# A two-block transformer kernel: modulation sums in column groups, and the pooling bias in one pass

## The reference, cut to what matters

```python
sc = jax.nn.silu(c)                                   # 1024 numbers
for i in range(DEPTH):                                # 2 layers
    mod = (sc @ ada_w[i] + ada_b[i]).reshape(B, N_MOD, D_MODEL)   # 9 x 1024
    x = modulated_sublayer(x, mod[:, 0:3], ..., swiglu ...)
    x = modulated_sublayer(x, mod[:, 3:6], ..., pool_mixer or mla_mixer ...)
    x = modulated_sublayer(x, mod[:, 6:9], ..., swiglu ...)

def modulated_sublayer(x, mod, g_pre, g_post, fn, weight):
    shift, scale, gate = mod[:, 0], mod[:, 1], mod[:, 2]
    h = rmsnorm(x, g_pre) * (1.0 + scale) + shift
    y = rmsnorm(fn(h), g_post)
    return x + weight * (1.0 + gate) * y
```

```python
y = jnp.einsum('bsgc,gcd->bsgd', pooled - hg, w) + b      # w (4,256,256), b (4,256)
return y.reshape(B, S, D_MODEL) * scale
```

## Time and profile before

| | |
|---|---|
| median of 3 runs | 1593.99 us (1592.29 to 1594.13) |
| the profiled execution, whole | 1589.41 us |
| its span, first to last instruction | 1587.6 us |
| busy in the span | PE 97%, DVE 78%, ACT 54%, POOL 5% |
| mean granted TensorE clock | 0.995 of full |
| chain that ended last | PE 88%, DVE 5%, ACT 4%, DMA 1%, issue 1% |

### The profile page before, as it was taken

One profiled execution on the slowest core, in us unless ns is written; L12 is line 12 of the kernel. 1 busy time (PEld: TensorE's weight loads), 2 busy tenths in 40 slices (PEclk: granted clock), 3 DMA queues, 4 the chain that ended last, 5 costly groups with the idle time before them and its releaser, 6 DMA issues.

```text
span 1587.6 us, 19436 instructions
## 1 busy us (share of the span) xinstructions
PE 1544.1 (97%) x7573; PEld 1255.5 (79%) x7573; DVE 1230.4 (78%) x1800; ACT 854.9 (54%) x1245; POOL 79.5 (5%) x135
## 2 busy tenths in 40 slices
PE   7999999999999999999999999899999999999998
PEld 3888886888888888877888888777788888787876
DVE  2898877988868888664486654759888799989896
ACT  3544445544445344456454543555567567777774
POOL 1110100000001000000011000000001000000000
PEclk9999999999999999999999999899999999999999
DMA  9999856988857988323267554345323569989893
GB/s 346 375 379 350 287 191 206 334 300 305 299 174 256 323 285 309 129 89 107 86 236 219 175 179 163 108 133 186 132 106 103 186 213 352 348 312 350 317 341 126
DMA packets 196338, 373.76 MB, mean 235 GB/s; under 512 B 8986, under 2 KB 102608, under 8 KB 196240
## 3 DMA queue, kind: packets, MB, share of 16 engines
q1 hardware_dynamic: 176688, 301.08, 55.0%
q0 software_dynamic: 18864, 69.76, 12.6%
q10 hardware_dynamic: 688, 1.62, 0.3%
HBM read 371.38 MB, written 1.05 MB: 235 GB/s over the span
## 4 chain that ended last, share of the span: by engine, by line
PE 88%; DVE 5%; ACT 4%; DMA 1%; issue 1%; SPq 0%; POOL 0%; DVEq 0%; ACTq 0%
PE banks L524 25%; PE banks L526 24%; PE banks L525 24%; DVE ul L460 1%; PE banks L1586 1%; PE banks L1067 1%; PE banks L635 1%; PE banks L1559 1%; ACT uh L449 1%; PE banks L2116 1%; DMA raw<-in_ffn_w_in 1%; PE banks L1573 1%; PE banks L2718 1%; ACT arena L762 1%; DVE full L1005 1%; PE banks L936 1%
## 5 line engine op out<-in xcount | busy, mean ns | idle before, releaser
L449 ACT ACTIVATE uh<-raw 128x1024 fp32r<-128x1024 f32 (+2 forms) x548 | 569.0, 1049 | 408.1 <-PE banks L526 403.3
L460 DVE TENSOR_TENSOR ul<-raw,uh 128x1024 fp32r<-128x1024 f32 (+2 forms) x548 | 656.8, 1209 | 163.3 <-ACT uh L449 155.3
L524 PE MATMUL banks<-uh,hh 128*128 128x512 f32 (+2 forms) x1296 | 514.7, 397 | 12.9 <-DVE hl L1011 8.1
L526 PE MATMUL banks<-uh,hl 128*128 128x512 f32 (+2 forms) x1296 | 502.9, 388 | 0.0
L525 PE MATMUL banks<-ul,hh 128*128 128x512 f32 (+2 forms) x1296 | 501.8, 387 | 0.0
L524 PEld LDWEIGHTS banks<-uh,hh 128*128 128x128 f32 x1296 | 244.3, 189 | 68.3 <-DVE hl L1011 11.5
L526 PEld LDWEIGHTS banks<-uh,hl 128*128 128x128 f32 x1296 | 244.1, 188 | 50.6
L525 PEld LDWEIGHTS banks<-ul,hh 128*128 128x128 f32 x1296 | 244.8, 189 | 46.3 <-issue 0.5
L524 PE MATMUL banks<-uh,bh 128*128 128x512 f32 x512 | 206.9, 404 | 0.9 <-DVE bl L2915 0.9
L526 PE MATMUL banks<-uh,bl 128*128 128x512 f32 x512 | 199.8, 390 | 0.0
L525 PE MATMUL banks<-ul,bh 128*128 128x512 f32 x512 | 199.4, 389 | 0.0
(11 more groups left out here) (356 smaller groups left out, 1288.0 us busy)
## 6 DMA issues: line engine op xcount, KB each, us to landing
raw<-in_ffn_w_in SPq DMA_DIRECT2D x176, 512.0 KB, 6.4
raw<-in_w_up SPq DMA_DIRECT2D x64, 1024.0 KB, 7.0
arena<-in_ada_w POOLq DMA_DIRECT2D x60, 1024.0 KB, 6.0
raw<-in_ffn_w_out SPq DMA_DIRECT2D x44, 1024.0 KB, 5.8
raw<-in_w_down SPq DMA_DIRECT2D x32, 1024.0 KB, 6.6
raw<-in_w_in SPq DMA_DIRECT2D x22, 1024.0 KB, 5.0
raw<-in_ada_w SPq DMA_DIRECT2D x12, 1024.0 KB, 11.0
raw<-in_w_mem_kv SPq DMA_DIRECT2D x4, 1024.0 KB, 5.4
```

The costliest lines, as they stand in the source:

```text
L449: act.e.activation(uh[r][:, 0:w], raw[m % NRAW][:, h * w:(h + 1) * w], AF.Copy).then_inc(act_done, ta.put("hi", u))
L460: dve.e.tensor_tensor(ul[r][:, 0:w], raw[m % NRAW][:, h * w:(h + 1) * w], uh[r][:, 0:w].bitcast(F32), ALU.subtract).then_inc(dve_done, tv. ...
L524: pe.e.matmul(o, a, wh, start=k + j == s0, stop=False)
L526: mm = pe.e.matmul(o, b, wh, start=False, stop=k + j == s1)
```

## The change

It has two parts.

**Modulation pieces of a shift or a scale.** The four matmuls with `acc` as stationary matrix go. In their place, within the next block's nine steps (behind the fourth of them), four matmuls with the stationary `ones[:, 0:32]` and the four quarters of `acc` as 128 moving columns each write to the four groups of 32 rows of bank 7. ACT copies the 128x128 result back to the first quarter of `acc`, and PE transposes it where the old sum stood; DVE reads columns 128, 160, 192 and 224 of bank 7. The weights of the steps change slightly (0.3 and 0.3 for 0.5). Where a block has a piece behind it and none of its own, one idle step stands before the sum and two behind it.

**Pooling bias.** POOL loads the four rows of bias and scale twice (rows 0 to 3 and 32 to 35), multiplies them, and writes a rounded high part and a low part to `gb`, a matrix of 128 rows that is zero elsewhere, beside four columns of ones for the choice of the group. PE's eight matmuls take `gb` in the float32r format (one pass) with all 128 rows. DVE's product L1426 goes.

```diff
-        def end_step_dve(dve, w, a, b):
-            yield w
-            ada_end_dve(dve, a, b)
-
+        def ada_rows(a):
+            return a is not None and not gate_piece(a)
+
+        SUM_STEP, ROW_STEP, COLUMN_STEP, GATE_STEP = 0.75, 0.3, 0.3, 1.3
+
+        def ada_idle(cur, k):
+            for _ in range(k if cur is not None else (1, 2)[k == 5]):
+                yield SUM_STEP
...
-            if gate_piece(a):
-                mm = pe.e.matmul(PB[b], ones[:, :], buf, start=True, stop=True)
+        def ada_steps_pe(pe, cur, old, b):
+            yield from ada_idle(cur, 4)
+            if ada_rows(old):
+                yield ROW_STEP
+                buf = acc[ADA_DVE.index(old) % 2]
+                pe.wait_ge(dve_done, tv("ada_s", old))
+                pe.take(b)
+                for g in range(4):
+                    mm = pe.e.matmul(PB[b][32 * g:32 * g + 32, 0:P], ones[:, 0:32], buf[:, g * P:(g + 1) * P],
+                                     start=True, stop=True)
+                mm.then_inc(pe_done, tp.put("ada_r", old))
+            yield from ada_idle(cur, 5)
...
+            if ada_rows(old):
+                yield COLUMN_STEP
+                pe.wait_ge(act_done, ta("ada_v", old))
+                pe.e.transpose(PB[b][:, P:2 * P], buf[:, 0:P], ident[:, :]).then_inc(pe_done, tp.put("ada_t", old))
             else:
-                mm = ada_columns_pe(pe, b, buf, ones[:, 0:1])
-            mm.then_inc(pe_done, tp.put("ada_t", a))
-            pe.frees(b, dve_done, tv, "ada_e", a)
+                yield GATE_STEP
+                pe.wait_ge(dve_done, tv("ada_s", old))
+                pe.take(b)
+                pe.e.matmul(PB[b], ones[:, :], buf, start=True, stop=True).then_inc(pe_done, tp.put("ada_t", old))
+            pe.frees(b, dve_done, tv, "ada_e", old)
+
+        def ada_steps_act(act, cur, old, b):
+            yield from ada_idle(cur, 4)
+            if ada_rows(old):
+                yield ROW_STEP
+                act.wait_ge(pe_done, tp("ada_r", old))
+                act.e.activation(acc[ADA_DVE.index(old) % 2][:, 0:P], PB[b][:, 0:P], AF.Copy).then_inc(
+                    act_done, ta.put("ada_v", old))
...
-            dve.e.tensor_tensor(pbb[0:4, :], pbb[0:4, :], psr[0:4, :], ALU.mult).then_inc(dve_done, tv.put("pb"))
...
-            pe.wait_ge(dve_done, tv("pb"))
+            pe.wait_ge(pool_done, tg("pb"))
...
-                    pe.e.matmul(PB[b][:, (g % 2) * 256:(g % 2) * 256 + 256], ident[0:4, g:g + 1].to_broadcast([4, P]),
-                                pbb[0:4, :], start=(g % 2 == 0), stop=False)
+                    pe.e.matmul(PB[b][:, (g % 2) * 256:(g % 2) * 256 + 256],
+                                gb[:, 256 + g:257 + g].to_broadcast([P, P]), gb[:, 0:256], start=(g % 2 == 0),
+                                stop=False)
...
+        def pool_rows_pool(pool):
+            def own():
+                pool.wait_ge(pool_done, tg.n)
+
+            pool.e.memset(gb[:, 0:260].bitcast(F32), 0.0).then_inc(pool_done, tg.put())
+            pool.wait_ge(loaded("ident"), 16)
+            pool.wait_ge(loaded("pool_rows"), 64)
+            for r in (0, 32):
+                v = pbb[r:r + 4, :]
+                own()
+                pool.e.tensor_tensor(v, v, psr[r:r + 4, :], ALU.mult).then_inc(pool_done, tg.put())
+            own()
+            pool.e.tensor_tensor(gb[0:36, 256:260], ident[0:36, 0:4], ident[0:36, 32:36], ALU.add).then_inc(
+                pool_done, tg.put())
+            for r in (0, 32):
+                own()
+                pool.e.tensor_copy(gb[r:r + 4, 0:256], pbb[r:r + 4, :]).then_inc(pool_done, tg.put())
+            own()
+            pool.e.tensor_tensor(gb[32:36, 0:256], pbb[32:36, :], gb[32:36, 0:256].bitcast(F32), ALU.subtract).then_inc(
+                pool_done, tg.put("pb"))
...
-            dve.wait_ge(loaded("pool"), 64)
+            dve.wait_ge(loaded("pool"), 32)
...
-            load("pool", pbb[0:4, :], I["pool_b"][0])
-            load("pool", psr[0:4, :], I["pool_scale"].rearrange("a (g n) -> (a g) n", n=256))
+            for r in (0, 32):
+                load("pool_rows", pbb[r:r + 4, :], I["pool_b"][0])
+                load("pool_rows", psr[r:r + 4, :], I["pool_scale"].rearrange("a (g n) -> (a g) n", n=256))
             load("pool", psb, I["pool_scale"].to_broadcast([P, D]))
+            pool_rows_pool(pool)
             pool.wait_ge(dve_done, tv("x", 0, 1))
```

More of the change, by code:

```diff
@@ L715, in ada_sums_dve @@
                     tv.same("ada_h", m)
-            yield 0.75
+                return
             dve.wait_ge(loaded("ident"), 16)
@@ L1173, in side @@
                     pe.later.add(idle(*FIRST_LATE))
-                if (i, s, b) in ADA_AT:
-                    pe.later.add(idle(*SUM_STEPS))
-                if (i, s, b - 1) in ADA_AT:
-                    pe.later.add(ada_sum_pe(pe, end_weight(ADA_AT[i, s, b - 1]), ADA_AT[i, s, b - 1], 7))
+                cur, old = ADA_AT.get((i, s, b)), ADA_AT.get((i, s, b - 1))
+                if cur is not None or old is not None:
+                    pe.later.add(ada_steps_pe(pe, cur, old, 7))
                 between(b)
@@ L1197, in side @@
                     act.later.add(idle(*FIRST_LATE))
-                if (i, s, b) in ADA_AT:
-                    act.later.add(idle(*SUM_STEPS))
-                if (i, s, b - 1) in ADA_AT:
-                    act.later.add(idle(end_weight(ADA_AT[i, s, b - 1])))
+                cur, old = ADA_AT.get((i, s, b)), ADA_AT.get((i, s, b - 1))
+                if cur is not None or old is not None:
+                    act.later.add(ada_steps_act(act, cur, old, 7))
                 between(b)
```

46 lines of the change are left out of this document (29 added, 17 removed).

## The result

The changed kernel takes 1584.82 us, the median of six runs (1583.19 to 1586.7), and the kernel before, timed beside it, 1592.36 (1590.69 to 1594.13, six runs, the three of the forecast among them): a ratio of 0.9955, 95% interval 0.9943 to 0.9966. The forecast was 1585.2 with 1579.0 to 1591.0.

What follows compares the result with a forecast made beforehand. PE was taken to bound the kernel (busy 97% of the span, 88% of the chain). Pieces 4.4, less 0.2 at the tenth, plus 4.6 at the pooling bias give 8.8 us: 1593.99 to 1585.2 us, range 1579.0 to 1591.0 (8 in 10).

Steps and rivals of the forecast that it cites:

- The new sum: Four column-group matmuls per piece on PE: 0.21 us streaming, 0.11 entering, 0.24 leaving, 0.56 us against 0.9 for the old sum.
- The transpose: PE's turn of each piece's copied sum, standing in the stream of products: 0.11 us each.
- The saving in a block: A piece costs PE 0.67 us and not 0.90: 0.23 us saved, 4.4 us for 19 pieces.
- The tenth piece: End of the first feed-forward sublayer, no products between sum and transpose: 0.96 us against 0.78, a loss of 0.18 us.
- The bias and the clock behind it: Pooling stage: one-pass bias matmuls save 2.8 us, and the clock fall behind them goes, 1.8 us; 4.6 us together.
- the rival of a clock that falls elsewhere: The clock still falls, at the pooling stage or elsewhere: gain only 7.0 us, time 1587.0 us; chance 0.20.
- The cover of ACT's copy: Products between sum and transpose hide ACT's copy, ready after 0.6 us; costed at nothing, 15 us if the cover were gone.
- DVE's room in the pooling stage: DVE's own work until L892 ends at 264.7 us, PE at 265.3: DVE is free 0.6 us before, costed at nothing.
- POOL's: POOL must have `gb` by 255.7 us and has 22 us for the landing and seven small instructions; costed at nothing.
- The last test that the prediction set itself: The prediction is wrong if the total of low clock in the run grows.
- the first two rivals: No cost for changing shape at the sums: 1578.6 us, chance 0.13; the clock still falls, there or elsewhere: 1587.0 us, chance 0.20.

Runs made afterwards that it cites:

- the two-pass kernel: The changed kernel with the eight bias matmuls taking the 128 rows of gb as plain float32, in two passes; 1591.89 us, one execution.

## Why the prediction was right

**The new sum** was put at 0.56 us and takes 0.557, and its parts hold: 0.22 of stream, 0.335 of entering and leaving (0.11 + 0.24 were read at L613). The reading from L613, whose passes have 512 columns, carried over because the price hangs on the visit and not on the length. **The transpose** was put at 0.11 and takes 0.121.

**The saving in a block** is the term that was mis-sized. 0.23 us a piece were forecast, and the blocks went from 17.70 (17.69 to 17.71) to 17.52 or 17.53 us, and 17.56 in the first of each row of them: 0.17 to 0.18 in most. The stream at the sum gained 0.34 and the transpose took 0.12 of it, as costed. The other 0.05 are products further on: of some 70 distances between products in a block, 13 are longer than 0.229 us (4 or 7 before), and their mean went from 0.2270 or 0.2273 to 0.2278 us. The prediction counted a stretch of three instructions and took the rest of the block as fixed. 19 pieces so gave 3.3 us and not 4.4.

**The tenth piece**: a loss of 0.18 was forecast, 0.25 stands in the trace. PE waits 0.40 us for ACT, as put down. The forecast's old count, 0.78 us, is the chain's and not the timeline's, which has 0.81 (1.03 less a product), and the transpose, which has no product ahead of it here, takes 0.17 (226.89 to 227.06) and not 0.11.

**The bias and the clock behind it**: 2.8 + 1.8 = 4.6 were forecast and the stage is 4.61 us shorter, with a clock of 1.00. About 0.1 of the 1.8 is the shape of the old passes, which slows the first pooling pass behind them too. The prediction named both what the rows are and how long the passes last; the two-pass kernel, in its one profile, shows that the rows do it. But this gain of the stage is not all a gain of the kernel. The forecast counted 1.8 us for a fall that goes and nothing for the others. One fall of 3.4 us less would raise the mean clock by 0.0011; over runs it is 0.99375 with the change and 0.99385 without, a difference of -0.0001 ± 0.0007: what one place gave back, others took. That is the rival of a clock that falls elsewhere (7.0 us), and the medians, 7.5 and 6.7 us apart in the two measurements, lie nearer to it than to the forecast's 8.8. At an equal clock the sum of both parts is 6.4 us, 3.1 of pieces and 3.3 of bias. The 3.3 ± 0.4 are not the passes alone: format and shape give 2.9, from which the 0.35 us at 478 us goes off, and the fall in this stage costs 1.7 us where the fit takes off only 1.4 for it (0.0011 of clock). That comes to some 2.9, an estimate.

**The cover of ACT's copy, DVE's room in the pooling stage and POOL's** were costed at nothing, and each was so, in the rows above. What the sum lacks is the 0.35 us that DVE starts late at 478 us.

The last test that the prediction set itself, that the total of low clock must not grow, came out against it in the first profile (22.7 us, 19.4 before) and for it in the second (19.1, 24.7 in the kernel before's second). One profile could not decide it. The prediction's range is a little tighter than its words: it is said to take in most of the first two rivals, and the first of them, 1578.6 us, lies just outside.

That 1585.2 stands so near to 1584.82 is in part luck: the difference was put at 8.8 us and is about 7.1, and the three runs that the forecast started from had a median 1.6 us above that of the comparison. The place of the gain was right in both parts; what failed to come in full is 1.1 us of the pieces and the clock's share of the bias.

## What to carry to other kernels

A visit to column groups has a fixed price, here 0.335 us, and four passes then go in the time of one; so collect the work of several small reductions into one visit, and each further one costs only its passes. A wait is worth nothing while products stand between its two ends, and its whole latency where none do: look at the last iteration of the loop first. Where a step's gain is in the clock, compare the mean granted clock over many runs before it is booked, for a fall that goes at one place may come back at another.

## What the runs showed of the hardware that was not expected

- Float32 matmuls with 4 of 128 rows, 3.6 us of them, have a fall of the clock to 1.2 GHz within them or right behind in four of four profiles; the same stretch with 128 rows, nearly all zero, leaves it at 2.4 GHz in its one profile, and nine other profiles without the 4-row passes agree.
- Eight passes with 36 rows among passes with 128 cost 0.38 us more than with 128: 0.09 on entering, 0.10 on the first of them, 0.09 on leaving and 0.10 on the first pass behind them. A visit to the column groups costs 0.335.
- The kernel with the pieces alone has a mean clock of 0.9923 over 22 runs, the kernel before and the one with both parts 0.9938; the cause is open.
- The mean clock explains most of the spread of a kernel's runs: 1.32 us for each 0.001, and 0.75 us of scatter around it, where the runs of the kernel before scatter by 1.75.
- One instruction of DVE at 478 us starts 0.35 us later in nine of the ten profiles with the new bias rows and in none of the four without; nothing edited stands near it, and the cause is open.
